# A two-block transformer step on one core: the first layer norm cut into two-tile pieces, table rows fetched two blocks ahead, weights laid out in 8 KB runs

## What is computed

```python
# block 0 (latent attention), for x and for ctx alike
h_lat = x * (1.0 + sc[:, None]) + sh[:, None]
y_lat, y_ctx = _mla_mixer(h_lat, h_ctx, cos, sin, mla_w_in[j], ...)     # ... @ w_out at its end
x = _layernorm(DEEPNORM_ALPHA * x + gt[:, None] * y_lat, ln_g[i], ln_b[i])
ctx = _layernorm(DEEPNORM_ALPHA * ctx + gt_c * y_ctx, ln_g[i], ln_b[i])
# block 1 (S5): the next modulation and the first projection read x and ctx again
h_lat = x * (1.0 + sc[:, None]) + sh[:, None]
u_l, g_l = jnp.split(h_lat @ w_in, 2, axis=-1)

def _layernorm(x, g, b):
    mu = jnp.mean(xf, axis=-1, keepdims=True)
    var = jnp.mean(jnp.square(xf - mu), axis=-1, keepdims=True)
    return (xf - mu) * lax.rsqrt(var + NORM_EPS) * g + b
```

## Time and profile before

| | |
|---|---|
| median of 3 runs | 1691.29 us (1687.27 to 1693.72) |
| profiled execution | 1694.61 us, span 1692.8 us |
| TensorE (PE) busy | 1552.3 us, 92% |
| VectorE (DVE) busy | 752.5 us, 44% |
| ScalarE (ACT) busy | 384.1 us, 23% |
| GpSimd (POOL) busy | 493.3 us, 29% |
| mean DMA rate | 187 GB/s |
| mean granted TensorE clock | 0.964 |

### The profile page before, as it was taken

The page is one execution under the profiler, slowest core; times in us unless marked ns, Lnnn a source line. Parts: engine busy times, 40 slices in busy tenths (PEclk is TensorE's granted clock), DMA queues, the critical chain, the costliest instruction groups (busy, mean ns, idle before and its releaser), DMA issues.

```text
span 1692.8 us, 26425 instructions
## 1 busy us (share of the span) xinstructions
PE 1552.3 (92%) x10366; PEld 1177.7 (70%) x10366; DVE 752.5 (44%) x1415; ACT 384.1 (23%) x871; POOL 493.3 (29%) x478
## 2 busy tenths in 40 slices
PE   5999899999999669998888899999999899999898
PEld 3444466665644358876666788888888788888787
DVE  6869566666577551256567100001171133433301
ACT  1144433333200020125454300000031011233301
POOL 0169999999871039412111000000000000000000
PEclk7999999999999789999999899999999999999999
DMA  9597778789899617649997544443443342444441
GB/s 387 162 295 252 214 156 207 168 213 224 198 259 241 229 29 171 254 162 320 303 325 237 161 152 154 157 156 125 149 150 109 115 149 100 150 149 149 142 137 69
DMA packets 211066, 316.51 MB, mean 187 GB/s; under 512 B 20128, under 2 KB 180000, under 8 KB 204960
## 3 DMA queue, kind: packets, MB, share of 16 engines
q1 hardware_dynamic: 176752, 220.74, 41.1%
q0 software_dynamic: 26672, 67.55, 16.5%
q10 hardware_dynamic: 7552, 26.96, 4.7%
HBM read 264.98 MB, written 50.20 MB: 186 GB/s over the span
## 4 chain that ended last, share of the span: by engine, by line
PE 51%; issue 2%; DVE 1%; ACT 0%; ACTq 0%; DVEq 0%; PEldq 0%
PE bank L829 26%; PE bank L1142 13%; PE bank L1033 3%; PE bank L1069 2%; PE bank L1209 2%; PE bank L1089 1%; PE bank L1047 1%; PE bank L1100 1%; PE bank L1081 0%; PE bank L1267 0%; PE bank L1254 0%; PE bank L1233 0%; PE bank L1198 0%; PE bank L1150 0%; PE bank L1052 0%
## 5 line engine op out<-in xcount | busy, mean ns | idle before, releaser
L829 PE MATMUL bank<-arena,ring 128*128 128x256 f32 x1312 | 286.4, 381 | 4.5 <-DVE arena L2410 4.5
L829 PEld LDWEIGHTS bank<-arena,ring 128*128 128x128 f32 x1312 | 250.4, 191 | 39.2 <-DVE arena L2410 4.9
L1142 PE MATMUL bank<-arena,ring 128*128 128x256 f32 x1024 | 223.9, 382 | 1.1 <-PEq L1133 1.1
L1142 PEld LDWEIGHTS bank<-arena,ring 128*128 128x128 f32 x1024 | 196.3, 192 | 28.3 <-issue 1.2
L829 PE MATMUL bank<-gate,ring 128*128 128x256 f32 (+1 forms) x640 | 197.4, 471 | 6.4 <-DVE gate L2305 3.4
L829 PEld LDWEIGHTS bank<-gate,ring 128*128 128x128 f32 x640 | 123.7, 194 | 79.6 <-issue 61.8
L829 PE MATMUL bank<-ht,ring 128*128 128x256 f32 (+1 forms) x544 | 175.0, 481 | 0.1
L829 PEld LDWEIGHTS bank<-ht,ring 128*128 128x128 f32 x544 | 102.6, 190 | 70.3 <-issue 61.1
L1010 PE MATMUL bank<-ring,ht 128*128 128x256 f32 x512 | 113.6, 383 | 11.9 <-DVE ht L1801 11.9
L1010 PEld LDWEIGHTS bank<-ring,ht 128*128 128x128 f32 x512 | 98.0, 192 | 25.6 <-issue 12.3
L2185 DVE SCALAR_TENSOR_TENSOR gate<-bank,col,gate 128x256 f32<-128x256 f32 x16 | 7.7, 482 | 196.4 <-ACT gate L1623 196.2
(11 more groups left out here) (381 smaller groups left out, 2290.0 us busy)
## 6 DMA issues: line engine op xcount, KB each, us to landing
ring<-in_s_w_glu SPq DMA_DIRECT2D x32, 1024.0 KB, 5.3
ring<-in_w_mod SPq DMA_DIRECT2D x24, 1024.0 KB, 12.7
ring<-in_w_up SPq DMA_DIRECT2D x22, 1024.0 KB, 5.1
ring<-in_s_w_in SPq DMA_DIRECT2D x16, 1024.0 KB, 10.3
arena<-s_b_powers SPq DMA_DIRECT2D x16, 1024.0 KB, 9.1
arena<-s_b_rows POOLq DMA_DIRECT2D x24, 512.0 KB, 11.5
arena<-s_power_rows POOLq DMA_DIRECT2D x24, 512.0 KB, 12.0
s_b_powers<-arena POOLq DMA_DIRECT2D x24, 512.0 KB, 5.9
```

The costliest lines, as they stand in the source:

```text
L829: mm = pe.matmul(psum[2 * (u % 2) + m][:, 0:mv.free_size()], ring[:, sl, k, m * P:(m + 1) * P], mv, start=(kg == 0 and k == 0), stop=(kg = ...
L1142: mm = pe.matmul(psum[4 * par + 2 * (s // 2) + m][:, 0:S], ring[:, sl, k, m * P:(m + 1) * P], yt[:, kg * 8 + k, :], start=(kg == 0 and k = ...
```

## The change

There are three parts.

**Rows.** `dve_rows` gets two more buffers, in the attention's probability tiles inside `ht`, which are free by then. ScalarE fetches the rows of n = 0 and n = 1 before the loop, and inside it those of n + 2.

**Layer norm.** VectorE adds tiles 0 to 5 of each half into `x_sum` after the residuals 0 to 2, so that TensorE's mean is one 512-wide matmul and four of 256. Subtraction, square and product go in pieces of two tiles (128x2x256), root and reciprocal by halves, and three of VectorE's eight modulations (k = 5 to 7) go to ScalarE.

**Layout.** All streamed weights are laid out before the launch, in the order of use, so that a partition's part of a unit is one 8 KB run, and a pair's attention weights are one DMA with runs of 5 KB. Bytes and units stay the same. Semaphore counts change with it.

```diff
+        dve_rows += [[carve(2048 * d + 1024 * z, 2, half // 2, base=hflat) for z in range(2)] for d in range(2)]
...
-            def load(slot, src):
-                sp.dma_start(ring[:, slot, 0:src.shape[1], 0:src.shape[2]], src).then_inc(w_in_[slot], 16)
+            def load(slot, name, n, k=8):
+                sp.dma_start(ring[:, slot].rearrange("p k m -> p (k m)")[:, 0:k * MT2],
+                             a[name][bass.ds(n, 1), :, 0:k * MT2].rearrange("a p x -> p (a x)")).then_inc(w_in_[slot], 16)
...
             def load_heads(p, b):
-                for c in range(2):
...
-                        sp.dma_start(att_uq[b][:, c, to:to + 2 * n].rearrange("p (h m) -> p h m", h=2), src[:, :, lo:lo + n])\
...
+                sp.dma_start(att_w[b], a["mla_heads"][bass.ds(p, 1)].rearrange("a p x -> p (a x)")).then_inc(att_in[b], 16)
...
-            def layer_sums():
-                pe.wait_ge(x_new, 16)
...
+            def first_layer_norm():
                 halves = ((xc, 0), (xl, S))
+                pe.wait_ge(row_sum, 1)
+                pe.matmul(psum[4][:, :], avg_d[:, :], x_sum, start=True, stop=False, skip_group_check=True)
+                for k in (6, 7):
+                    pe.wait_ge(x_new, 2 * (k + 1))
+                    for x, lo in halves:
+                        mm = pe.matmul(psum[4][:, lo:lo + S], avg_d[:, :], x[:, k, :], start=False, stop=(k == 7), skip_group_check=True)
                 mm.then_inc(ln_stat, 1)
                 for h, (x, lo) in enumerate(halves):
                     for k in range(KD):
+                        if k % 2 == 0:
+                            pe.wait_ge(ln_sq, 4 * h + k // 2 + 1)
+                        mm = pe.matmul(psum[5 + h][:, lo:lo + S], avg_d[:, :], ht[:, k, lo:lo + S], start=(k == 0), stop=(k == KD - 1))
+                    mm.then_inc(ln_stat, 1)
...
             table_rows(0, 1)
             act.dma_start(dve_c.rearrange("p n z d q c -> p n (z d q c)"), a["s5_c"][:, N_POOL:NB5, :]).then_inc(dve_c_in, 16)
+            for d in range(2):
+                table_rows(1, d)
...
-                    if n + 1 < N_DVE:
-                        table_rows(n + 1, d)
+                    if n + 2 < N_DVE:
+                        table_rows(n + 2, d)
...
+            for h, (x, lo) in enumerate(halves):
+                for c in range(4):
+                    act.wait_ge(ln_centered, 4 * h + c + 1)
+                    act.activation(ht[:, 2 * c:2 * c + 2, lo:lo + S], x[:, 2 * c:2 * c + 2, :], ACT.Square).then_inc(ln_sq, 1)
+            for h, (x, lo) in enumerate(halves):
+                act.wait_ge(ln_stat, 2 + h)
+                root(ln_rs[:, lo:lo + S], psum[5 + h][:, lo:lo + S])
             act.wait_ge(mod_set, 5)
             for k in range(KD):
+                act.wait_ge(ln_norm, k // 2 + 1)
                 modulate(1, k)
+            for k in range(LAT_DVE, KD):
...
                 residual(i, s, 0, True, at, u0, i, i + (at + 2 * s + 2))
...
+                if n < 3:
+                    for lo, x in ((0, xc), (S, xl)):
+                        v = x_sum[:, lo:lo + S]
+                        if n == 0:
+                            link.post(tt(v, x[:, 0, :], x[:, 1, :], ALU.add))
...
             for x, lo in ((xc, 0), (xl, S)):
-                tt(x[:, :, :], x[:, :, :], psum[4][:, lo:lo + S].unsqueeze(1).to_broadcast([P, KD, S]), ALU.subtract)\
-                    .then_inc(ln_centered, 1)
+                for c in range(4):
+                    pair_of_rows(x, c, psum[4][:, lo:lo + S], ALU.subtract).then_inc(ln_centered, 1)
+            for h, (x, lo) in enumerate(((xc, 0), (xl, S))):
+                dve.wait_ge(root_set, 3 + h)
+                link(dve.reciprocal(ln_rs[:, lo:lo + S], ln_rs[:, lo:lo + S]))
+                for c in range(4):
+                    pair_of_rows(x, c, ln_rs[:, lo:lo + S], ALU.mult).then_inc(ln_norm, 1)
+            for k in range(LAT_DVE):
...
+    h["mla_out"] = units(inputs["mla_w_out"][0], groups=2)
```

More of the change, by code:

```diff
@@ L248, in program @@
         rot_t = c1(S)
-        att_uq = [c1(2, 2 * HQ) for _ in range(2)]
-        att_uk = [c1(2 * NOPE) for _ in range(2)]
-        att_uv = [c1(2 * VDIM) for _ in range(2)]
+        att_w = [c1(HW) for _ in range(2)]
+        att_uq = [w[:, 0:4 * HQ].rearrange("p (c m) -> p c m", c=2) for w in att_w]
+        att_uk = [w[:, 4 * HQ:4 * HQ + 2 * NOPE] for w in att_w]
+        att_uv = [w[:, 4 * HQ + 2 * NOPE:HW] for w in att_w]
         at_heads = c1.at
@@ L444, in program @@
         cp_stored = sem("cp_stored")
-        dve_rows_in = [sem(f"dve_rows{i}_in") for i in range(2)]
+        dve_rows_in = [sem(f"dve_rows{i}_in") for i in range(4)]
         dve_c_in = sem("dve_c_in")
@@ L622, in _ @@
                 sp.wait_ge(slot_done, at + s - NSLOT + 1)
[L623 removed]
+                load((at + s) % NSLOT, "mod_tail", s)
             with turns(sp, 6, 2) as i:
@@ L708, in _ @@
                 sp.wait_ge(y_done, NB5 + s - 3)
-                load((at + s) % NSLOT, rows8(wg, s % 2, s // 2 * E_BR))
+                load((at + s) % NSLOT, "glu", s)
             sp.wait_ge(yt_set, NB5 + 1)
@@ L2087, in _ @@
                 dve.sem_inc(unit_free[(u0 + s) % 2], 2)
+                if n < 3:
[3 more added lines that the diff above has]
+                            link.post(tt(v, x[:, 0, :], x[:, 1, :], ALU.add))
+                        else:
+                            link.upto(1)
+                            link.post(tt(v, v, x[:, 2 * n, :], ALU.add))
+                    if n:
+                        for lo, x in ((0, xc), (S, xl)):
+                            v = x_sum[:, lo:lo + S]
+                            link.upto(1)
+                            link.post(tt(v, v, x[:, 2 * n + 1, :], ALU.add))
+                    if n == 2:
+                        link.upto(0)
+                        dve.sem_inc(row_sum, 1)
             for d in range(2):
@@ L2589, in rows, with blocks, units @@
         return w.reshape(k // P, P, m).transpose(1, 0, 2).reshape(P, k // P * m)
+    def blocks(w, at, groups=1):
+        out = np.zeros((len(at) * groups, P, 8 * MT2), np.float32)
+        for n, c0 in enumerate(at):
+            for g in range(groups):
+                part = rows(w[g * 8 * P:(g + 1) * 8 * P, c0:c0 + MT2])
+                out[n * groups + g, :, 0:part.shape[1]] = part
+        return out
+    def units(w, lo=0, hi=None, groups=1):
+        return blocks(w, range(lo, hi or w.shape[1], MT2), groups)
     cols = np.zeros((P, NVT * P), np.float32)
```

178 lines of the change are left out of this document (82 added, 96 removed).

## The result

The changed kernel takes 1676.41 us (median of 5 runs, 1674.71 to 1679.28) against 1687.74 us of the kernel before on the same chip (5 runs, 1687.27 to 1693.72). The ratio on record, formed over the runs, is 0.9919, 95% interval 0.9892 to 0.9946; the two medians alone give 0.9933, inside it. That is 0.8% faster (11 us between the medians) where 1.9% (32 us) was forecast, and the time lies above the range that was given (1645 to 1671 us). Its profiled execution took 1679.05 us, with a span of 1677.2 us and a mean granted clock of 0.971.

A forecast was written before the change was run, and what follows sets the result against it. TensorE was taken to bound nearly every stretch, except 560 to 600 us, where it waits for late tables and the norm's chain. Gains 14.9 + 15.1 + 2 = 32.0 us gave 1659 us, range 1645 to 1671.

The forecast's parts named there:

- Part 1: Output projection: with rows fetched ahead, the last residual ends at 570.3 instead of 585.2 us, a gain of 14.9 us.
- The step within part 1: VectorE's tables: without row waits it finishes at 566.6 us, before TensorE's projection, which then ends last.
- a store must land in 13.6 us after its issue: VectorE's table buffers: a store must land before the block after overwrites its buffer, 13.6 us later.
- Rival B: Tables: ScalarE's queue sets the pace; gain 2.1 us instead of 14.9, 1672 us, half the effect 1665; chance 0.17.
- VectorE at its first residual at 512.6: Output projection: VectorE reaches its first residual at about 512.6 us, the time read from the kernel before.
- ScalarE's packets should pass faster: Output projection's DMA: a weight unit in 8 KB packets holds up 128 of ScalarE's packets instead of 1024.
- The front, 0 us: Attention: its weights in one DMA lie beside softmax work, so 0 gained, at most a few us.
- Part 3: Norm, from last residual to S5 projection: 18.9 us instead of 34.0, a gain of 15.1 us, bounds 13 to 16.
- S5 loop, 2 us: S5 loop: 8 KB weight runs shrink the 26.7 us of "issue" gaps by 5 to 10%, about 2 us.
- Rival C: S5 loop: gaps shrink by half, 13 us instead of 2, giving 1648 us; chance 0.15.
- The rule on 512 B: Weight DMA: line rate from 512 B on, so 1 KB and 8 KB runs cost the same; kept as a rival.
- Rival E: S5 loop: instruction fetches take longer turns with 8 KB weight packets; no change or slower, about 1702 us; chance 0.04.

The follow-up runs named there:

- gate_8k: The kernel before with only the ten weight units of the S5 loop in 8 KB runs; 0.9931 of the kernel before.
- late_rows: The changed kernel with the rows of n = 1 fetched behind the first block's b stores instead of before the loop; 0.9917 of the kernel before.
- rows_by_sp: The changed kernel with the rows of n = 1 fetched through SP's queue, after the fourth weight unit of mla_out; 0.9935 of the kernel before.
- stores_first: The changed kernel with rows of n = 1 fetched behind block 0's b store, rows of n + 2 behind n's c store; 0.9897 of the kernel before.
- front_stores: The changed kernel with the edits of front_1k and stores_first together; 0.9886 of the kernel before.
- after_again: The changed kernel run once more, nothing altered; 0.9957 of the kernel before.
- out_1k: The changed kernel with only the output projection's weights (mla_out) back in 1 KB runs; 0.9905 of the kernel before.
- front_out_1k: The kernel of front_1k with the output projection's weights in 1 KB runs as well; 0.9921 of the kernel before.
- layout_norm: The kernel before with the layout and the norm in pieces, rows one block ahead with two buffers; 0.9875 of the kernel before, 1669.82 us.
- front_1k: The kernel of layout_norm with the weights of mla_gate and mod_tail in 1 KB runs; 0.9869 of the kernel before.
- gate_1k: The kernel of layout_norm with the ten weight units inside the S5 loop in 1 KB runs; 0.9916 of the kernel before.
- front_gate_1k: The kernel of front_1k with the ten weight units of the S5 loop in 1 KB runs as well; 0.9881 of the kernel before.
- front_1k_2: The kernel of front_1k run once more, nothing altered; 0.9837 of the kernel before, 1662.74 us.
- rows_norm: The kernel before with rows two blocks ahead and the norm in pieces, weights in 1 KB runs; 0.9926 of the kernel before.

## Why the prediction was wrong

The twenty profiles (both first ones and the eighteen experiments), read at the places that matter. A range is lowest to highest over the kernels of that kind. A single profile is not much to go by: `gate_8k` runs the same program as the kernel before up to the S5 loop, with its last residual at 578.71 instead of 585.20.

| | 1 KB runs there | 8 KB runs there |
|---|---|---|
| attention starts (front weights) | 186.6 to 197.9, median 189.1 (10) | 193.1 to 201.4, median 195.5 (10) |
| first row fetch issued to first table (`mla_out`) | 16.4 to 19.6 us (6) | 20.1 to 35.5 us in 13, 15.8 in one |
| S5 projection to gate projection (loop units) | 320.5 to 325.4 us, median 321.9 (5) | 308.8 to 322.9 us, median 314.6 (15) |

**Step by step.**

- *Part 1, 14.9 us: failed, and it is the step that broke the forecast.* The last residual was to end at 570.3 and ended at 592.25, 22.0 us later. Of these, 7.3 are the later start of the projection (below). 5.6 are the projection itself: 117.2 us instead of 111.6, since TensorE waited 3.88 us for the late first residual and then took 58.10 us for a half instead of 55.20 (granted clock 0.59 from 523 to 530 us, 1.00 behind that). The last 9.1 come because the residual ends 10.8 us after the projection instead of 1.7.
- *The step within part 1: that VectorE, rid of the row waits, runs free.* It waited 14.2 us for stores, and without them it would have been done at 578.0, before TensorE's 581.43. The condition was written down (a store must land in 13.6 us after its issue), though the median was already 16.3, and then judged by the sum of engine shares; the longest c store now took 23.3. What decides which transfer is late is the order of the queue. Ahead of and with the c store that the second block's b table waits for, the kernel before puts two fetches of 1 MB, 0.5 MB of c, the b store, 1 MB of rows and the store itself: 4.5 MB. The change puts 6.5 MB there. ScalarE's queue moved 16.58 MB in 131 us, 0.127 MB a microsecond, so 2 MB more are up to 16 us, an estimate. The wait was 10.65 us, and 16.11, 11.09, 10.88, 14.07 and 13.99 in the other kernels with this order; with 1 MB taken away (`late_rows`) 5.44; 0 to 2.2 in the kernels with 4.5 MB (4.06 in `rows_by_sp`, where the other 2 MB go through SP's queue). The slowest b store says the same: 20.9 to 30.6 us to landing in those six, 8.0 to 17.4 in the ten kernels with rows one block ahead.
- *What reordering gave back: the wait, not the time.* `stores_first` and `front_stores` (4.5 MB again) are rid of that wait, and their last residual still ends 10.0 and 7.7 us after the projection, because rows come late instead. Rival B (ScalarE's queue sets the pace, 0.17) named the place, a wait for stores in the b tables. That its price, 12.8 us less gain, is near the 14.7 that were lost is partly luck, since 5.6 of these are not VectorE's waits. With rows one block ahead and 8 KB runs in `mla_out` the last residual ends 1.7 to 2.2 us after the projection in four profiles, 5.9 to 6.9 in three.
- *VectorE at its first residual at 512.6 "as before": wrong by 9 us* in this execution (521.57), by 2 in `after_again` (514.43). The rows for it were issued 7.3 us later and took 35.5 us instead of 17.4; the table shows that 8 KB weights in `mla_out` go with late rows (13 of 14 profiles above the highest of the six with 1 KB), and `out_1k` and `front_out_1k` that giving only these weights their 1 KB runs back brings the rows sooner. "ScalarE's packets should pass faster" had the sign wrong: taken one for one, as in the earlier trace rows (174 against 183) and after the change (287 against 269), a 4 KB packet gets the smaller part beside one of 8 KB. The prediction read the row only for the time at the end of a unit. One for one is no rule, either: from 460 to 480 us the kernel before moved 388 against 1336.
- *The front, 0 us: a term that was missing.* "The attention weights in one DMA: 0" looked at those weights alone, not at mla_gate and mod_tail, whose 8 KB packets share with the stores that the attention waits for. In eight of ten profiles with 1 KB runs it starts before 190, in none of ten with 8 KB. Taking it out gave 0.9957 and 0.9919 to 0.9896 in the changed kernel, and 0.9875 and 0.9901 to 0.9869 and 0.9837 without rows ahead, 6 to 7 us both times; each of these differences is little more than its noise, some 5 us, but both point the way that the starts of the attention do. Two profiles with 1 KB start at 197.6 and 197.9: something else can delay it too, and that was not found.
- *Part 3, 15.1 us: right in mechanism, 12.7 measured.* From the subtraction on all is as worked out: 595.45 to the S5 projection is 18.1 us, forecast 18.9 - 1.2 = 17.7. The mean took 3.2 us instead of 1.2. TensorE had waited 9.24 us before it, and its granted clock from 591 to 596 us is 0.50 (1.2 GHz) and a pair of matmuls takes 1.06 us. In `layout_norm`, where it had been busy until then, the clock is 1.00 from 581 to 585 and a pair takes 0.59. There the norm takes 19.4 us. Over all profiles it is 32.4 to 36.0 us in the old form (4) and 19.4 to 23.4 in the new (16). The highest, 23.3 and 23.4 (`out_1k`, `front_1k`), show the wait that is next: the subtraction waits 5.25 and 5.31 us for the last c store.
- *S5 loop, 2 us: right in place, too small; 10.0 measured, 7.3 between the medians.* Rival C had said 13, all of it from shorter gaps of kind "issue". These do shrink: 26.7 us before, 26.0 in `gate_1k` and 23.9 in `front_gate_1k`, but 16.9 in the changed kernel, 8.0 in `layout_norm` and 5.7 in `front_1k_2`. Much of it is given back as waits for `s_responses` (6.2, 15.9 and 19.3 us), and in `gate_8k` nearly all: 14.2 us of gaps and 11.7 of those waits, in its profiled execution, its slowest, with a stage of 322.0. The other half of the gain is not in the waits at all. The loop alone, first before, then after (stretch, its us, TensorE's busy time and instructions, granted clock, DMA share, GB/s):

```profile
758.30:926.90 168.60, 141.86 (x2860) 0.92 0.95 299
```
```profile
752.80:911.10 158.30, 136.70 (x2860) 0.95 0.96 313
```

Of 10.3 us, 5.2 are TensorE's own work, the same 2860 matmuls at a higher granted clock. Over all profiles they take 141.1 to 142.8 us in the five with 1 KB runs in the loop (clock 0.90 to 0.92) and 134.2 to 141.6 in the fifteen with 8 KB (0.91 to 0.97). No term of the forecast had this, and what lets the clock rise was not tested. Timed, the ten units bring 11 us in `gate_8k` against before, 2 in `gate_1k` and about 5 in `front_gate_1k`, of which only the first is clear of the noise. So that the 8 KB runs shorten the loop is well supported; by how much, 2 to 11 us, and by what path is open.

- *The rule on 512 B* (Trainium skill, "DMA: Bandwidth & Descriptors", Specifications) speaks of line rate. From 457 to 588 us SP's queue moved 10.49 MB at 26.5%, 3.31 us of all engines for one MB, where it had been 4.3 and 2.41 was forecast. So larger runs did cost less here, though by half of the forecast. The same page's Queues, rings and completion order says that an engine goes round the queues by packet, and that such a packet holds several descriptors, so it need not be what the profile counts as one. The rows of 460 to 480 us after the change come out one for one (287 against 269), those before do not (1336 against 388).
- *Rival E (slower by longer turns)* was near the mechanism, at the wrong place: what shares with the 8 KB runs does get slower, in the front and at the first rows, but the "issue" gaps got smaller.

**Where the gain went.** Of 32.0 us forecast on the span 15.6 came: 14.7 less from part 1, 7.3 lost ahead of the projection, 2.4 less from the norm, 8.0 more from the S5 loop. Rows two blocks ahead, put on top of layout and norm, cost 0.005 (mean 0.9938 against 0.9888), 8 us, and 0.004 (0.9896 against a mean of 0.9853) with the front repaired. The first is clear of its noise (0.003), though the kernels ran on different chips, the second only just; where 1 KB runs are kept, rows ahead cost nothing and give nothing (0.9999). The fastest kernel is the change without its rows part and with the front weights in 1 KB: 0.9869 and 0.9837, 1.3% to 1.6% faster than before, against 0.4% to 0.8% for the change as made.

**Open.** Why the attention starts at 198 in two profiles with 1 KB runs; the size of the S5 loop's gain, and why TensorE's clock is higher there; why rows two blocks ahead cost time even where the store wait is gone (`front_stores`); and whether rows ahead would help with the stores on a queue of their own, which was not tried.

## What to carry to other kernels

A fetch that is issued earlier stood here in front of what the same queue was given after it: add up the bytes ahead of the transfer that is waited for next, not only the load of the engines. Reordering alone may just move the wait. Larger runs made their own queue faster here and one that shares the engines slower, so try them on the transfers that are late, and small runs on those that have time. A wait that is removed shows the one behind it, here a store behind the mean of the norm.

## What was not expected of the hardware

- A DMA issue on ScalarE, 0.6 us before, took up to 10.87 us (12.36 in `after_again`) once several fetches of 512 KB stood in its queue; ScalarE's next instruction began only when it ended.
- VectorE's operations of 128x512 took 0.69 us where GpSimd stood still and mostly 1.58 to 1.75 where it computed beside them. Before, GpSimd computed most of the time from 486 to 514 us, ahead of VectorE's first residual; after, it waited 11.32 us for a store, until 505.99, and had finished by 512.
- After 9.24 us without work TensorE did the few matmuls of the mean at half its clock, which lengthened that chain by 2 us; the granted clock was still 0.78 on the squares behind it (596 to 606 us), and 1.00 there in `layout_norm` (585 to 593).
- The start of the output projection moved between 456.1 and 473.1 us over the profiles, by as much as the effects that were sought. Part of it does not reach the end: with 457.0 and 473.1 (kernel before and `rows_norm`) the last residual ended at 585.2 and 585.8.
